# Gate and lift products of three branches with tokens on the output partitions

## The chip, the cores and the metric

One NeuronCore of a Trainium2 chip runs the whole program. The metric is the device time of one execution in microseconds (us). The engines are TensorE (PE; its weight loads are shown apart as PEld), VectorE (DVE), ScalarE (ACT), GpSimd (POOL) and SyncE (SP), which here issues the transfers of the weights.

## What is computed

Two encoder layers (DEPTH 2) on 256 tokens with a model width of 2048, in float32. A layer projects x, runs three token mixers (S5 scan, Hyena convolution, latent attention), each with 1024 channels, and merges them:

```
proj = x @ w_in[i]                      # 2048 wide into all branches, gates and PLE logits
y_a, y_b, y_c = three mixers, each times silu of its own part of proj      # 256 x 1024 each
gates  = sigmoid(gate_logits)           # 256 x 3 x 2048
lifted = y_n @ w_lift[n]                # 256 x 2048 for each branch n
mixed  = sum over n of gates_n * lifted_n, then @ w_out[i]
ple    = (p[i] @ w_ple[i]) * sigmoid(ple_logits)
x      = layer_norm(ALPHA * x + mixed + ple, ln_g[i], ln_b[i])
```

The change is in gates, lifted and the sum over the branches, and in how that sum reaches the product with w_out.

## The kernel before

**Weights.** All large weights come as 184 blocks a layer of 128 partitions x 2048 float32 (1 MB), in halves, through a ring of four half slots. ACT copies each quarter (128x512) of a block rounded to fp32r into WH (make_wh, L374), DVE subtracts it from the raw quarter into WL (make_wl, L388). x is held the same way as XH and XL (together XX), with channels on partitions and tokens as columns. A product is three fp32r matmuls: high x high, low x high, high x low. WH and WL hold one block; quarter q of the next block can be made only when TensorE is done with quarter q of this one (parts_used), so ACT and DVE run about three quarters ahead of TensorE at most.

**Narrow blocks.** A gate block holds the 2048 x 128 weights of 128 output channels. whole_block (through half_block, L1554) has the weight tile stationary and 256 tokens of x moving: 16 contraction tiles x 3 matmuls of 256 columns = 48 matmuls into one bank, channels on the output partitions. A lift block holds the 1024 x 128 weights of two output tiles: two half_block calls, again 48 matmuls of 256 columns. So the order of a layer is gate, gate, lift, eight times for each branch (24 blocks a branch, 48 gate and 24 lift blocks a layer).

**Merging.** For each pair of gate tiles ACT applies the sigmoid (into GA) from banks 0 and 1, and DVE multiplies by the lifts in banks 2 and 3. Branch A writes MIX; branches C and B multiply into LM and add to MIX (mix_in and its copy in the loop, L1058, L1060, L1114, L1116). MIX has channels on partitions.

**Stages of a layer**, in the order of each engine's hand-written program: S5 with the other projections; "lifta", where the 24 blocks of branch A are laid around the attention of eight heads (scores, block 3h, transposes of the probabilities, block 3h+1, product with V, block 3h+2); "hyc", 24 blocks of branch C around the Hyena filters and convolutions; "lift", 24 blocks of branch B in a hardware loop of two turns with little else; "ple", ten narrow blocks of the PLE logits and then 64 float32 matmuls for p @ w_ple; "out", the product with w_out; layer norm.

**Already wide.** The out stage has tokens on the output partitions: out_step takes 128 tokens of MIXH or MIXL as stationary tile and a 512-column quarter of WH or WL as moving one, 24 matmuls of 512 columns for a block, into banks 2g and 2g+1 for the two token halves. It takes MIX with channels on partitions; in "ple", ACT copies all of it to MIXH (L1461, 128x4096) after block 0 and DVE makes MIXL (L1122, 128x4096) after block 1. RES (ALPHA times x, L1126 and L1129) is made in four pieces at blocks 3 to 6.

**Between hyc and lift** ACT copies the Hyena result to YBH (L1441, 128x2048) and DVE makes YBL (L1098) before the weight splits of the second lift-stage block.

Of the kernel before, what the change touches and what calls it, by code (L numbers as in the profile page):

```python
# [27 lines left out]
F32 = mybir.dt.float32  # L28
# [6 lines left out]
P = 128  # L35
# [69 lines left out]
    "lifta": [8, 8, 8, 8, 0, 0, 0, 0],  # L105

    "hyc":  [8, 8, 8, 8, 18, 18, 20, 18],

    "lift": [8, 8, 8, 8, 0, 0, 0, 0],
    "ple":  [5, 5, 8, 8, 0, 0, 0, 0],  # L110
# [67 lines left out]
def trunk(nc, x, blocks, lp, ln, bc, w1, w2, b3, decay, feats, pT, pos, angles, consts, out):  # L178
    with ExitStack() as ctx:
# [103 lines left out]
        GA, LM = split(area(65, 2), 2), split(area(67, 2), 2)  # L283
        PTI = area(45, 2)
        MIXH, MIXL = parts("MIXH", 90, 16), parts("MIXL", 106, 16)
        RES = area(0, 16)
# [40 lines left out]
        mix_ready, ples_ready = sem("mix_ready"), sem("ples_ready")  # L327
# [91 lines left out]
        def _(pool):  # L419
# [7 lines left out]
            with pool.Fori(0, DEPTH) as layer:  # L427
# [27 lines left out]
                pool.wait_ge(yl_ready, layer * 4 + 1)  # L455
# [46 lines left out]
        def _(dve):  # L502
# [61 lines left out]
            with dve.Fori(0, DEPTH) as layer:  # L564
# [310 lines left out]
                dve.wait_ge(yh_ready, layer * 4 + 1)  # L875
                v.tensor_tensor(YAL, U, YAH.bitcast(F32), ALU.subtract).then_inc(yl_ready, 1)

                dve.wait_ge(yl_ready, layer * 4 + 1)
# [32 lines left out]
                for h in range(HEADS):  # L911
# [35 lines left out]
                    for b in range(2):  # L947
                        out_of(b, "lifta", h)
                        full(2 + b, "lifta", h)
                        free(v.tensor_tensor(split(MIX, DT)[:, 2 * h + b, :], GA[:, b, :], bank[2 + b][:, 0:T], ALU.mult), 2 + b)  # L950
                for b in (2, 3):
                    out_of(b, "lifta", 7)
# [99 lines left out]
                def mix_in(i, stage, n):  # L1052

                    for b in range(2):
                        mix = MIX[:, (2 * i + b) * T:(2 * i + b + 1) * T]
                        out_of(b, stage, n)
                        full(2 + b, stage, n)
                        free(v.tensor_tensor(LM[:, b, :], GA[:, b, :], bank[2 + b][:, 0:T], ALU.mult), 2 + b)  # L1058
                        out_of(2 + b, stage, n)
                        v.tensor_tensor(mix, mix, LM[:, b, :], ALU.add).then_inc(mix_ready, 1)  # L1060

                for k in range(24):
# [5 lines left out]
                    if s_ == 1 and o == 0:  # L1068

                        dve.wait_ge(yh_ready, layer * 4 + 2)  # L1070
                        v.tensor_tensor(YCL, YC, YCH.bitcast(F32), ALU.subtract).then_inc(yl_ready, 1)
# [20 lines left out]
                    if k % 3 == 2:  # L1092
                        mix_in(k // 3, "hyc", k // 3)
# [3 lines left out]
                dve.wait_ge(yh_ready, layer * 4 + 3)  # L1097
# [3 lines left out]
                with dve.Fori(0, 2) as turn:  # L1101
                    for k in range(12):
                        make_wl(dve, v, layer, B_LIFT + 48 + k + 1, turn, 12)
                        if k == 0:

                            dve.wait_ge(mix_ready, layer * 32 + 16)
                        if k % 3 < 2:
                            continue
                        for b in range(2):
                            i = k // 3  # L1110
                            mix = MIX[:, bass.ds(turn * (8 * T) + (2 * i + b) * T, T)]
                            out_of(b, "lift", i + turn * 4)
                            full(2 + b, "lift", i + turn * 4)
                            free(v.tensor_tensor(LM[:, b, :], GA[:, b, :], bank[2 + b][:, 0:T], ALU.mult), 2 + b)  # L1114
                            out_of(2 + b, "lift", i + turn * 4)
                            v.tensor_tensor(mix, mix, LM[:, b, :], ALU.add).then_inc(mix_ready, 1)  # L1116

                for m in range(10):
                    make_wl(dve, v, layer, B_PLE + m + 1)
                    if m == 1:  # L1120
                        dve.wait_ge(yh_ready, layer * 4 + 4)
                        v.tensor_tensor(MIXL, MIX, MIXH.bitcast(F32), ALU.subtract).then_inc(yl_ready, 1)  # L1122
                    if 3 <= m < 7:
                        half = slice((m % 2) * 8 * T, (m % 2 + 1) * 8 * T)
                        if m < 5:
                            st.did(v.tensor_scalar(RES[:, half], XH[:, half].bitcast(F32), ALPHA, None, ALU.mult))  # L1126
                        else:
                            st.wait()
                            st.did(v.scalar_tensor_tensor(out=RES[:, half], in0=XL[:, half].bitcast(F32), scalar=ALPHA, in1=RES[:, half],  # L1129
                                                          op0=ALU.mult, op1=ALU.add))  # L1130
# [86 lines left out]
        def _(act):  # L1217
# [11 lines left out]
            with act.Fori(0, DEPTH) as layer:  # L1229
# [153 lines left out]
                for h in range(HEADS):  # L1383
# [9 lines left out]
                    for b in range(2):  # L1393
                        for half in range(2):
                            make_wh(act, half, layer, lift_a(3 * h + 1 + b))
                        if h == b == 0:

                            act.wait_ge(qk_ready, layer * 2 + 2)
                        full(b, "lifta", h)

                        act.wait_ge(psum_free[2 + b], nth(layer, "lifta", 2 + b, h))
                        free(a.activation(GA[:, b, :], bank[b][:, 0:T], ACT.Sigmoid), b)
# [6 lines left out]
                for k in range(24):  # L1409
# [3 lines left out]
                    if k == 0:  # L1413

                        out_of(7, "mla", 7)
                        full(3, "lifta", 7)
# [16 lines left out]
                    b, i = k % 3, k // 3  # L1433
                    if b < 2:
                        full(b, "hyc", i)

                        act.wait_ge(psum_free[2 + b], nth(layer, "hyc", 2 + b, i))
                        free(a.activation(GA[:, b, :], bank[b][:, 0:T], ACT.Sigmoid), b)
# [4 lines left out]
                with act.Fori(0, 2) as turn:  # L1443
                    for k in range(12):
                        for half in range(2):
                            make_wh(act, half, layer, B_LIFT + 48 + k + 1, turn, 12)
                        b, i = k % 3, k // 3
                        if b < 2:
# [681 lines left out]
```

## Time and profile before

| | us |
|---|---|
| median of 3 runs | 2745.6 (2743.52 to 2748.16) |
| the profiled execution | 2739.96 |
| its span | 2737.7 |
| TensorE matmuls busy | 2634.4 (96%) |
| VectorE busy | 1886.8 (69%) |
| ScalarE busy | 1301.2 (48%) |
| mean granted TensorE clock | 0.985 |

Busy time of TensorE counts overlapped matmuls as one stretch, and the duration printed for one matmul includes its pipeline. The time that a matmul costs in a stream is therefore read from start to start. A timeline row is: start, duration, engine, line, operation, output <- inputs, shape, count, and in brackets the idle time before it and who ended it. A windows row is: stretch, its length, busy time and count for PE, PEld, DVE, ACT and POOL, the granted clock, the share of the DMA engines, GB/s.

### The profile page before, as it was taken

The page shows a single profiled execution, that of the slowest core. Times are in us where ns is not written, and L with a number is a line of the kernel's source. Part 1 is how long each engine was busy: PE and PEld are TensorE (multiplying, and loading weights), DVE is VectorE, ACT ScalarE, POOL GpSimd, SP SyncE. Part 2 cuts the span into 40 slices and gives each one's busy share as a digit, 9 for nine tenths or more (in the row PEclk, how much of TensorE's full clock was granted, in tenths as well). Part 3 has the DMA queues.
Part 4 walks back from the last instruction along what each step waited for, and adds up shares of the span by engine and source line. Part 5 has one row for each costly group of instructions (what it writes and reads, how often), then busy time and mean ns, then how long its engine had stood idle before and what let it go on. Part 6 is the DMA issues. An engine that isn't in the chain of part 4 may idle for free.

```text
span 2737.7 us, 48913 instructions
## 1 busy us (share of the span) xinstructions
PE 2634.4 (96%) x17128; PEld 2340.3 (85%) x17128; DVE 1886.8 (69%) x3381; ACT 1301.2 (48%) x2350; POOL 112.2 (4%) x206
## 2 busy tenths in 40 slices
PE   7999999999999999999989999999999999999998
PEld 6889999888987778998778999988799878789986
DVE  7788787635675767566678778786266757665666
ACT  5555555634543333453465555555355433344535
POOL 2100000000000000000030000000000000000000
PEclk9999999999999999999999999999999999999999
DMA  7444444334453324555464444443344523245554
GB/s 249 157 151 152 152 144 157 130 134 144 145 173 101 124 91 149 183 177 170 162 204 155 150 149 149 151 146 124 140 153 140 170 85 128 97 160 183 175 173 146
DMA packets 115978, 412.19 MB, mean 151 GB/s; under 512 B 15460, under 2 KB 15514, under 8 KB 115584
## 3 DMA queue, kind: packets, MB, share of 16 engines
q1 hardware_dynamic: 107424, 391.17, 43.0%
q0 software_dynamic: 8416, 19.18, 2.1%
q8 instruction: 88, 1.44, 0.2%
q14 instruction: 50, 0.41, 0.0%
HBM read 403.99 MB, written 6.29 MB: 150 GB/s over the span
## 4 chain that ended last, share of the span: by engine, by line
PE 86%; DVE 7%; issue 3%; ACT 2%; DMA 1%; PEldq 0%; PEld 0%; DVEq 0%; POOL 0%; POOLq 0%; ACTq 0%; SPq 0%
PE bank L1554 31%; PE bank L1582 19%; PE bank L1584 9%; PE bank L1924 6%; PE bank L1536 5%; PE bank L1672 2%; PE bank L1654 2%; PE bank L1635 2%; DVE WL L388 1%; PE bank L1845 1%; PE bank L1620 1%; PE bank L1740 1%; PE bank L1825 1%; PE bank L1807 1%; PE bank L1764 1%
## 5 line engine op out<-in xcount | busy, mean ns | idle before, releaser
L374 ACT ACTIVATE WH<-ring 128x512 fp32r<-128x512 f32 x1364 | 855.6, 631 | 1210.9 <-PE bank L1554 574.1
L388 DVE TENSOR_TENSOR WL<-ring,WH 128x512 fp32r<-128x512 f32 x852 | 571.1, 688 | 466.8 <-ACT WH L374 464.4
L1582 PE MATMUL bank<-XX,WH 128*128 128x512 f32 x2304 | 821.7, 400 | 26.7 <-DVE XX L557 15.2
L1554 PE MATMUL bank<-XX,WH 128*128 128x256 f32 x3712 | 687.4, 287 | 12.7 <-DVE WL L388 8.3
L1584 PE MATMUL bank<-XX,WL 128*128 128x256 f32 x2304 | 644.7, 280 | 0.0
L1554 PEld LDWEIGHTS bank<-XX,WH 128*128 128x128 f32 x3712 | 584.2, 194 | 31.4 <-issue 23.9
L1582 PEld LDWEIGHTS bank<-XX,WH 128*128 128x128 f32 x2304 | 436.0, 189 | 128.2 <-DVE XX L557 15.2
L1554 PE MATMUL bank<-XX,WL 128*128 128x256 f32 x1856 | 528.2, 285 | 0.0
L379 DVE TENSOR_TENSOR WL<-ring,WH 128x512 fp32r<-128x512 f32 x512 | 350.7, 687 | 137.8 <-ACT WH L374 133.8
L1584 PEld LDWEIGHTS bank<-XX,WL 128*128 128x128 f32 x2304 | 437.6, 190 | 0.0
L1554 PEld LDWEIGHTS bank<-XX,WL 128*128 128x128 f32 x1856 | 359.1, 193 | 0.0
L1536 PE MATMUL bank<-ARENA,ring 128*128 128x256 f32 x704 | 159.0, 388 | 13.9 <-ACT ARENA L1345 11.0
L1536 PEld LDWEIGHTS bank<-ARENA,ring 128*128 128x128 f32 x704 | 134.1, 194 | 38.4 <-issue 16.2
L1924 PE MATMUL bank<-WL,MIXH 128*128 128x512 f32 x256 | 101.9, 398 | 0.0
L1924 PE MATMUL bank<-WH,MIXH 128*128 128x512 f32 x256 | 101.1, 395 | 0.0
L1924 PE MATMUL bank<-WH,MIXL 128*128 128x512 f32 x256 | 101.0, 395 | 0.0
L1554 PE MATMUL bank<-YCH,WH 128*128 128x256 f32 x256 | 79.1, 309 | 0.0
L1554 PE MATMUL bank<-YCH,WL 128*128 128x256 f32 x256 | 75.0, 293 | 0.0
L1554 PE MATMUL bank<-YCL,WH 128*128 128x256 f32 x256 | 75.0, 293 | 0.0
L1554 PE MATMUL bank<-YAH,WH 128*128 128x256 f32 x256 | 75.0, 293 | 0.0
L1554 PE MATMUL bank<-YAH,WL 128*128 128x256 f32 x256 | 71.9, 281 | 0.0
L1554 PE MATMUL bank<-YAL,WH 128*128 128x256 f32 x256 | 71.9, 281 | 0.0
(305 smaller groups left out, 3492.4 us busy)
## 6 DMA issues: line engine op xcount, KB each, us to landing
ring<-in_blocks SPq DMA_DIRECT2D x738, 512.0 KB, 3.3
ARENA<-in_bc POOLq DMA_DIRECT2D x2, 2048.0 KB, 8.7
ARENA<-in_decay POOLq DMA_DIRECT2D x8, 512.0 KB, 4.3
ARENA<-in_x SPq DMA_DIRECT2D x4, 512.0 KB, 8.1
u_scratch<-ARENA POOLq DMA_DIRECT2D x16, 128.0 KB, 2.3
ARENA<-u_scratch POOLq DMA_DIRECT2D x64, 32.0 KB, 2.9
y_scratch<-ARENA POOLq DMA_DIRECT2D x16, 128.0 KB, 2.0
ARENA<-y_scratch POOLq DMA_DIRECT2D x64, 32.0 KB, 2.7
```

The source lines that it names most:

```text
L374: nc.scalar.activation(wh[q], raw(which[0], q), ACT.Copy).then_inc(wh_ready[q], 1)
L379: nc.vector.tensor_tensor(wl[q], raw(which[0], q), wh[q].bitcast(F32), ALU.subtract).then_inc(w_used[slot(which[0], q // 2)], 1)
L388: vec.tensor_tensor(wl[q], raw(which[0], q), wh[q].bitcast(F32), ALU.subtract).then_inc(w_used[slot(which[0], half)], 1)
L1536: ins = mm(o, w[:, (w0 + i) * P:(w0 + i + 1) * P], rhs(i), start=i == 0, stop=i == k - 1)
L1554: ins = mm(o, w_, x_, start=start and i == 0 and n == 0, stop=stop and i == 7 and n == 2)
L1582: ins = mm(bank[b][:, :], h, xx[:, :, k, :], start=(k == 0), stop=(k == DT - 1), skip_group_check=True)
L1584: ins = mm(bank[b][:, 0:T], l, xh[:, k, :], start=False, stop=(k == DT - 1), skip_group_check=True)
L1620: ins = nc.tensor.transpose(bank[b][:, i * P:(i + 1) * P], part_of(E, i % 2, i // 2, q, P), ident)
L1635: ins = mm(o, ET[:, q % 2 * CW + i * P:q % 2 * CW + (i + 1) * P], u4(q), start=True, stop=True)
L1654: ins = mm(bank[b][:, at:at + P], w_, f, start=(q % 2 == d == r == 0), stop=(q % 2 == d == r == 1), skip_group_check=True)
L1672: ins = mm(o, f, x_, start=False, stop=(d == 1 and r == 1))
L1924: ins = mm(bank[b][:, :], x_[:, k, tok[t]], w_[q], start=False, stop=(k == 15 and n == 2), skip_group_check=True)
```

## The change

Gate and lift products of the three branches take the form of the out stage. The host lays the weights out as blocks of four contraction tiles x 512 output channels (rows_by_cols). Output channels go in four groups of 512; a group has four gate blocks, accumulating in banks 0 and 1 (one for each half of the tokens), then two lift blocks in banks 2 and 3: six blocks in place of the six of two old rounds, and the same 24 blocks and bytes a branch. A block is token_block: for each quarter three matmuls of 512 columns for either token half, 24 in all. Sigmoid, product and sum work on 128x512 (two of each for six blocks, where four of 128x256 stood), and LM is gone: the product is written back to GA.

MIX now has tokens on partitions. 32 transposes a layer turn it back, 16 after PLE block 1 and 16 after block 4, four to a bank of banks 4 to 7. ACT rounds each bank into 512 columns of MIXH and DVE subtracts into MIXL, two banks at each of PLE blocks 2, 3, 5 and 6; the two 128x4096 operations are gone. The pieces of RES move to blocks 1, 4, 7 and 8, and the sigmoid of the first six PLE tiles from block 3 to block 7. The waits for YAL, YCL and YBL move from the third block of a branch to the fifth.

```diff
+                def token_step(b, x, k, t, q, first, last):
+
+                    hi, lo = (part[:, k, token[t]] for part in x)
+                    for n, (x_, w_) in enumerate(((hi, wh), (lo, wh), (hi, wl))):
+                        ins = mm(bank[b][:, :], x_, w_[q], start=first and n == 0, stop=last and n == 2)
+                        if n < 2:
+                            release(ins)
+                    return ins
+
+                def token_block(b, x, j, n, *which):
+
+                    for q in range(4):
+                        part_made(q, *which)
+                        k = 4 * j + q
+                        ins = [token_step(b + t, x, k, t, q, k == 0, k == 4 * n - 1) for t in range(2)]
...
+                def gated_block(stage, g, p, x, y, *which):
+
+                    b = 0 if p < 4 else 2
+                    if p in (0, 4):
+                        for t in range(2):
+                            take_bank(b + t, stage, g)
+                    token_block(b, y if b else x, p - 4 if b else p, 2 if b else 4, *which)
...
-                    take_bank(0, "lifta", h)
-                    whole_block(0, xh, xl, lift_a(3 * h))
+                    attention = lambda k: gated_block("lifta", k // 6, k % 6, (xh, xl), (split(YAH, WT), split(YAL, WT)), lift_a(k))
+                    attention(3 * h)
...
+                def mix_in(g):
+
+                    for t in range(2):
+                        out_of(t, "hyc", g)
+                        full(2 + t, "hyc", g)
+                        free(v.tensor_tensor(GA[:, t, :], GA[:, t, :], bank[2 + t][:, :], ALU.mult), 2 + t)
+                    for t in range(2):
+                        out_of(2 + t, "hyc", g)
+                        v.tensor_tensor(mix_part(g, t), mix_part(g, t), GA[:, t, :], ALU.add).then_inc(mix_ready, 1)
...
-                    if k % 3 == 2:
-                        mix_in(k // 3, "hyc", k // 3)
+                    if k % 6 == 5:
+                        mix_in(k // 6)
...
+                    if m in (1, 4):
+                        pe.wait_ge(mix_ready, layer * 16 + 16)
+                        for n in range(4 * (m // 4), 4 * (m // 4) + 4):
+                            b = 4 + n % 4
+                            take_bank(b, "ple", n // 4)
+                            for i in range(4):
+                                at = i % 2 * D + (2 * n + i // 2) * P
+                                ins = nc.tensor.transpose(bank[b][:, i * P:(i + 1) * P], MIX[:, at:at + P], ident)
...
+                        for n in mix_pairs[m]:
+                            full(4 + n % 4, "ple", n // 4)
+                            a.activation(MIXH[:, n * CW:(n + 1) * CW], bank[4 + n % 4][:, :], ACT.Copy).then_inc(mixh_ready, 1)
```

## Rows read from the trace of the kernel before

**Rows 1.** The page: busy time of the engines, chain that ended last by engine
```profile
PE 2634.4 (96%) x17128; PEld 2340.3 (85%) x17128; DVE 1886.8 (69%) x3381; ACT 1301.2 (48%) x2350; POOL 112.2 (4%) x206
PE 86%; DVE 7%; issue 3%; ACT 2%; DMA 1%; PEldq 0%; PEld 0%; DVEq 0%; POOL 0%; POOLq 0%; ACTq 0%; SPq 0%
```

**Rows 2.** Windows: two hyc gate blocks; a lift-stage round; four out blocks; ten PLE blocks
```profile
834.54:846.15 11.61, 11.61 (x98) 11.61 (x97) 8.31 (x13) 4.67 (x8) 0.98 (x2) 1.00 0.29 92
1088.83:1105.97 17.14, 17.14 (x146) 17.14 (x145) 9.65 (x17) 8.14 (x14) 0.00 (x0) 1.00 0.57 185
1292.37:1314.86 22.49, 22.49 (x99) 18.06 (x97) 13.76 (x28) 9.62 (x16) 0.00 (x0) 1.00 0.57 189
1193.59:1253.33 59.74, 58.31 (x481) 57.74 (x481) 39.17 (x49) 31.68 (x51) 0.00 (x0) 1.00 0.53 176
```

**Rows 3.** Timeline of PE, lift stage: first matmuls of gate pair, lift block, next pair
```profile
1088.83 0.40 PE L1554 MATMUL bank<-XX,WH 128*128 128x256 f32 x2
...
1100.34 0.28 PE L1554 MATMUL bank<-YBH,WH 128*128 128x256 f32 x1
...
1105.97 0.40 PE L1554 MATMUL bank<-XX,WH 128*128 128x256 f32 x2
```

**Rows 4.** Timeline of PE, out stage: first two matmuls of a group, next group's transposes
```profile
1292.37 0.48 PE L1924 MATMUL bank<-WH,MIXH 128*128 128x512 f32 x1
1292.69 0.40 PE L1924 MATMUL bank<-WH,MIXL 128*128 128x512 f32 x1
...
1314.86 0.49 PE L1939 MATMUL bank<-CON,ARENA 128*128 128x128 f32 x3
```

**Rows 5.** Timeline of PE, S5 stage: 512-column matmul on XX, the next matmul
```profile
204.11 0.39 PE L1582 MATMUL bank<-XX,WH 128*128 128x512 f32 x1
204.34 0.28 PE L1584 MATMUL bank<-XX,WL 128*128 128x256 f32 x1
```

**Rows 6.** Timeline of PE, attention: starts and ends of blocks 3h and 3h+2 of a head
```profile
651.88 0.50 PE L1554 MATMUL bank<-XX,WH 128*128 128x256 f32 x2
...
657.74 0.60 PE L1773 MATMUL bank<-CON,ARENA 128*128 128x128 f32 x4
...
664.60 0.47 PE L1554 MATMUL bank<-YAH,WH 128*128 128x256 f32 x1
...
670.49 0.38 PE L1763 MATMUL bank<-ARENA 128*128 128x256 f32 x1
```

**Rows 7.** Timeline of PE, S5 stage: 16 transposes and what follows them
```profile
90.66 1.89 PE L1635 MATMUL bank<-ARENA 128*128 x16
92.39 1.04 PE L1620 MATMUL bank<-CON,ARENA 128*128 128x128 f32 x8
```

**Rows 8.** Timeline of PE and of DVE where lift follows hyc
```profile
1055.15 0.80 PE L1554 MATMUL bank<-XX,WH 128*128 128x256 f32 x2 [2.82 <-DVE WL L388]
1060.23 0.36 PE L1554 MATMUL bank<-XX,WH 128*128 128x256 f32 x1 [0.50 <-DVE WL L388]
...
1055.62 0.41 DVE L1058 TENSOR_TENSOR ARENA<-ARENA,bank 128x256 f32<-128x256 f32 x1
...
1057.20 2.28 DVE L1098 TENSOR_TENSOR YBL<-ARENA,YBH 128x2048 fp32r<-128x2048 f32 x1
1059.40 0.68 DVE L388 TENSOR_TENSOR WL<-ring,WH 128x512 fp32r<-128x512 f32 x1
```

**Rows 9.** Timeline of DVE, lift stage: from the end of a round to the next splits
```profile
1106.96 0.69 DVE L388 TENSOR_TENSOR WL<-ring,WH 128x512 fp32r<-128x512 f32 x1 [0.77 <-ACT WH L374]
1107.57 0.41 DVE L1114 TENSOR_TENSOR ARENA<-ARENA,bank 128x256 f32<-128x256 f32 x1
...
1109.38 1.29 DVE L388 TENSOR_TENSOR WL<-ring,WH 128x512 fp32r<-128x512 f32 x2
```

**Rows 10.** Timeline of DVE and PE in ple: the large subtraction and who waits
```profile
1207.16 4.42 DVE L1122 TENSOR_TENSOR MIXL<-ARENA,MIXH 128x4096 fp32r<-128x4096 f32 x1
...
1212.33 0.47 PE L1554 MATMUL bank<-XX,WH 128*128 128x256 f32 x2 [0.85 <-DVE WL L388]
```

More of the change, by code:

```diff
@@ L946, in _ @@
                     short_conv(3 * h + 2)
[L947 to L950, printed above, removed]
+                    for t in range(2) if h % 2 else ():
+                        g = h // 2
+                        out_of(t, "lifta", g)
+                        full(2 + t, "lifta", g)
+                        free(v.tensor_tensor(mix_part(g, t), GA[:, t, :], bank[2 + t][:, :], ALU.mult), 2 + t)
                 for b in (2, 3):
-                    out_of(b, "lifta", 7)
+                    out_of(b, "lifta", 3)
                 out_of(7, "mla", 7)
@@ L1104, in _ @@
                         if k == 0:
-                            dve.wait_ge(mix_ready, layer * 32 + 16)
-                        if k % 3 < 2:
+                            dve.wait_ge(mix_ready, layer * 16 + 8)
+                        if k % 6 < 5:
                             continue
[L1109 to L1116, printed above, removed]
+                        i = k // 6
@@ L1784, in _ @@
                     done(ins, 7)
-                    if h == 0:
-                        pe.wait_ge(yl_ready, layer * 4 + 1)
-                    for i in range(2):
-                        take_bank(2 + i, "lifta", h)
-                        done(half_block(bank[2 + i][:, 0:T], i, split(YAH, WT), split(YAL, WT), True, True, lift_a(3 * h + 2)), 2 + i)
+                    attention(3 * h + 2)
                 settle()
@@ L1863, in inverse @@
                         done(ins, b)
-                def lift_blocks(stage, n, b, hi, lo, first, *which):
-                    if b < 2:
-                        take_bank(b, stage, n)
-                        whole_block(b, xh, xl, *which)
-                        return
-                    if first is not None:
-                        pe.wait_ge(yl_ready, first)
-                    for i in range(2):
-                        take_bank(2 + i, stage, n)
-                        done(half_block(bank[2 + i][:, 0:T], i, hi, lo, True, True, *which), 2 + i)
-                hi, lo = split(YCH, WT), split(YCL, WT)
+                yc = (split(YCH, WT), split(YCL, WT))
                 for k in range(24):
@@ L1894, in _ @@
                         inverse(o, s_ - 10)
-                    lift_blocks("hyc", k // 3, k % 3, hi, lo, layer * 4 + 2 if k == 2 else None, B_LIFT + 24 + k)
-                hi, lo = split(YBH, WT), split(YBL, WT)
+                    if k == 4:
+                        pe.wait_ge(yl_ready, layer * 3 + 2)
+                    gated_block("hyc", k // 6, k % 6, (xh, xl), yc, B_LIFT + 24 + k)
+                yb = (split(YBH, WT), split(YBL, WT))
                 settle()
```

154 lines of the change are left out of this document (90 added, 64 removed).

## Prediction

> **What bounds the kernel now.** First the page: matmuls keep TensorE busy for 96% of the span, it has 86% of the chain that ended last, VectorE 7% [rows 1]. So time is won where TensorE issues less or waits less, and work of ScalarE and VectorE counts only where TensorE stands waiting behind it. Then the windows of single stages, because the stages have different limits [rows 2]. In a round of the lift stage (gate, gate, lift) TensorE is busy for all of 17.14 us, VectorE for 9.65, ScalarE for 8.14, and the transfers take 0.57 of the DMA engines. The out stage looks the same with 22.49 us for four blocks and the same 0.57. The granted clock, the third column from the end, is 1.00 in both. Both are bounded by TensorE alone. In the ten PLE blocks 59.74 us hold only 58.31 of matmul time, so some waits stand there. Last, the timeline, start to start, for the price of one matmul, since the printed durations overlap.
>
> **The price of a block, narrow and wide.** In the lift stage a pair of gate blocks runs from 1088.83 to 1100.34, 11.51 us, 96 matmuls of 256 columns: 120 ns each, 5.755 us a block. The lift block runs from 1100.34 to 1105.97, 5.63 us, 48 matmuls: 117 ns each [rows 3]. The wide form exists in the out stage: 96 matmuls of 512 columns from 1292.37 to 1314.86. The first gap, 0.32 us, holds a switch from transposes of about 0.09; the rest is (22.49 - 0.09) / 96 = 233.3 ns each, 5.60 us for a block of 24 [rows 4]. Columns are the same in sum (48 x 256 = 24 x 512), so the gain is what a matmul costs above its columns: 5.755 - 5.60 = 0.155 us for a gate block and 0.03 for a lift block. The new instructions are those of the out stage in shape, order and moving operand; only the stationary tile is cut from XX, YAH, YBH or YCH, which no row shows. The price could be anything from 230 ns (the 512-column matmul with XX moving, 204.11 to 204.34 [rows 5]) to twice the gate's 120, 240. I take 233.3, the row nearest to the new form.
>
> The Trainium skill (TensorE: Matmul & The Clock Gate, "Wait — 56ns, not 53.3ns?") gives a warm matmul its columns at 2.4 GHz plus about 2.5 ns. By that two narrow ones would cost 2.5 ns more than one wide one, 0.06 us a block, 8.6 us for the 144 blocks. The trace gives 6.7 ns for a gate pair (2 x 120 - 233.3) and 1.3 for a lift pair, and neither width costs as little as the rule says. It returns beside a rival below.
>
> **Gain, stage by stage** (each number for both layers).
> - Lift stage: a round of 17.14 [rows 2] becomes 3 x 5.60 = 16.80, so 0.34 less, in 16 rounds: 5.4 us.
> - Attention: block 3h takes 651.88 to 657.74, 5.86 us, and block 3h+1, between the other two, 5.84; block 3h+2 takes 664.60 to 670.49, 5.89 [rows 6]. Above 48 matmuls these hold a switch from other work of 0.10, 0.08 and 0.26. With the out stage's 0.09 for the first two and 0.20 for the third, the new ones are 5.69, 5.69 and 5.80. That is 17.59 - 17.18 = 0.41 a head, in 16 heads: 6.6 us.
> - Hyc: a pair of gates between other work takes 11.61 [rows 2]; new 11.20 + 0.09, so 0.32 less, eight pairs' worth of gates a layer, 16 in both: 5.1 us. 16 lift blocks at 0.03 give 0.5. In two places of each layer TensorE stands for the last unconv of VectorE, which starts from the middle of a block; there half a block's gain (0.07) is lost, 0.2 in all. 5.4 us.
>
> Sum 17.4 us.
>
> **Added: 64 transposes.** In the S5 stage 16 float32 transposes take 90.66 to 92.39, 1.73 us, 108 ns each [rows 7]. A burst of 16 with one switch of 0.09 is 1.82, four bursts 7.3 us, all of it on TensorE in the PLE stage, where nothing hides it. The ends: the 275 ns that one of them is busy if nothing overlapped (1.89 - 15 x 0.108 = 0.27), 17.6 us, and about 6.4 at 100 ns. At the first burst TensorE also waits for the last sum into MIX, but two whole PLE blocks (11.5 us) lie ahead of it, and VectorE is done with the sums some 4 us after the lift stage; so nothing. The second burst needs banks 4 to 7 free again, read by VectorE at blocks 2 and 3, about 3 us after the end of block 3 and 2.5 before the transposes. Behind these waits only TensorE's own blocks are queued. The SP queue is not passed by any moved step; the blocks are as many and as large.
>
> **Removed: the large copies.** The copy to MIXH and the 4.42 us subtraction to MIXL hold back the splits of PLE block 2 and 3; TensorE waits, 0.85 us of it marked [rows 10]. Ten blocks at 5.755 would be 57.55 and they take 59.74 [rows 2]. Of the 2.2 left 0.7 is at the seam to the next stage (a wait for a transfer), and layer 1 has 59.12 without it, so 1.4 us a layer is the cost of the large operations: 2.8 us gained. In their place at blocks 2, 3, 5 and 6 stand two copies and two subtractions of 128x512, some 0.6 and 0.7 us each, behind the quarter that comes last (1.6 us after a block's end). The next quarter is then ready about 3.8 us after the block's end, and TensorE wants it at 5.76. The subtractions of RES (2.3 us each) sit at blocks 7 and 8, alone, as at 5 and 6 before. If this cover failed I would see TensorE idle there, up to the 1.4 us again.
>
> **Added: a longer stand at the seam from hyc to lift.** TensorE waits there on the low parts anyway, 2.82 and then 0.50 us (from 1059.57 to 1060.23 at the matmul starts) [rows 8]. VectorE's chain is: last splits, four sums of 128x256 (1055.62 to 1057.20, 1.58 us), YBL 2.2 us, split of the next block at 1059.40. Four operations of 128x512 at the 0.61 at which such splits follow each other take 2.5 us in place of 1.58: YBL, the split and TensorE come 0.9 later, in both layers 1.9 us lost. The move of the wait for YBL to the fifth block brings nothing: YBL is done 6 us before its old place.
>
> **Hidden: the sums elsewhere.** In the lift stage the last quarter's split ends at 1107.57, 1.60 us after the round ended (1105.97), four narrow operations take 1.81 and the next split starts at 1109.38 [rows 9]. Wide: 2.5 to 2.8 us, the next quarter ready at 1110.7 to 1111.0, wanted at 1105.97 + 5.60 = 1111.57. At least 0.5 us of cover is left. In attention the products end 0.5 us later ahead of every second softmax, which has over a microsecond in hand; the sigmoids fall on every second head alone.
>
> **The sum.** -17.4 + 7.3 - 2.8 + 1.9 = -11.0 us. Against the profiled execution, 2739.96, that is 2729.0. It lies 5.6 below the median; in the same ratio the median of 2745.6 becomes 2734.6.
>
> **Rivals.**
> - Width gives less on XX: a wide matmul there costs 236.6 ns, halfway between the out stage's 233.3 and twice the gate's 120. That is 2304 x 3.3 ns = 7.7 us less gain, 2742.3. For it: the lift blocks, already at 117 ns, gain next to nothing. Against: the out stage [rows 4] and XX moving at 230 [rows 5]. Chance 0.09. The Trainium skill's rule from the section named above ends near the same time by another road, 8.6 us of gain in place of 17.4 and so 2743.4; the traces speak against it, since neither width has its gap here.
> - XX as an operand costs 120 ns for 256 columns wherever it stands, so its wide matmul costs 240. Its place: the 96 gate blocks, 2304 matmuls, 6.7 ns each: 15.4 us more than forecast, 2750.0, slower than before. It turns from faster to slower at 238 ns. For it: YBH in the same loop has 117 where XX has 120. Against: XX moving over 512 columns takes 230 [rows 5]. Chance 0.07.
> - The wide sums use up their cover, and TensorE waits at every sixth block of hyc and lift (16 places); this decides from a chain of 3.3 us, and at 0.5 us each it costs 8: 2742.6. Chance 0.06.
> - More stands go than I count (softmax chain, PLE blocks, switches as cheap as 0.09 everywhere, a seam hidden), 6 us more: 2728.6. Chance 0.10.
> - The clock falls in other places: after the stand of 2.82 us a pair of matmuls shows 0.80 us where others have 0.40 to 0.50 [rows 8, 3], the lower of the two levels (1.2 GHz). One more or one less in each layer moves the time by 3 to 4 us either way, inside the range.
> - The change not doing what it says is ruled out by its diff: every narrow block of the three branches is replaced.
>
> **Chances.** The forecast has 0.68, and of it 0.95 lies below the bound. 0.2% of the median, about what a measurement of this kernel can tell from no change, is 5.5 us: faster means below 2740.1. Faster: 0.65 + 0.10 = 0.75, and a small part of the two middle rivals, 0.77. Slower by over 0.2% (above 2751.1): a third of the second rival and what I have not thought of, 0.05. Same: 0.18. The range that leaves out 2 in 10 is 2728 to 2743.
>
> **What would show it.** In the changed trace: 512-column matmuls on XX 233 ns apart and a lift-stage group of six blocks in 33.6 us (two old rounds: 34.3); 16 transposes in about 1.7 us, twice a layer; no wait for a split within the PLE blocks; the first wait of the lift stage unchanged and the second one near 1.5 us in place of 0.66; every six-block end without a wait. The forecast is wrong if matmuls on XX are 237 ns or more apart, if the transposes take over 3 us a burst, or if TensorE waits for low parts behind the wide sums.

## The result, and the profile after

| us | before | after |
|---|---|---|
| median (range, runs) | 2744.85 (2743.52 to 2748.16, 4) | 2709.48 (2707.26 to 2712.84, 4) |
| the profiled execution | 2739.96 | 2707.26 |
| its span | 2737.7 | 2705.7 |
| TensorE matmuls busy | 2634.4 | 2605.2 |

The ratio is 0.9874, 95% interval 0.9861 to 0.9886: 35 us faster, between 31 and 38. The forecast was 2734.6, 11 us faster, and its range ended at 2728. The sign was right and the size a third of what came.

The page of the changed kernel, the same two lines as [rows 1]: busy time, then the chain that ended last.

```profile
PE 2605.2 (96%) x13736; PEld 2160.3 (80%) x13736; DVE 1882.6 (70%) x3315; ACT 1275.7 (47%) x2300; POOL 111.3 (4%) x206
PE 90%; DVE 5%; issue 2%; ACT 2%; DMA 1%; PEldq 0%; PEld 0%; DVEq 0%; POOL 0%; POOLq 0%; ACTq 0%
```

TensorE is still the bound, with 3392 fewer matmuls. Windows of the changed kernel (columns as in [rows 2]): four gate blocks of the lift stage, two lift blocks, four out blocks, the ten PLE blocks with the transposes, the first four gate blocks after the seam, the taps behind hyc block 2, then the stages attention, hyc of layer 0 and hyc of layer 1.

```profile
1075.17:1096.98 21.81, 21.81 (x98) 18.02 (x96) 13.19 (x21) 10.12 (x16) 0.00 (x0) 1.00 0.61 193
1131.24:1142.44 11.20, 11.20 (x49) 9.01 (x48) 5.57 (x9) 5.92 (x10) 0.00 (x0) 1.00 0.52 188
1253.13:1275.61 22.48, 22.48 (x100) 18.05 (x98) 12.46 (x28) 9.49 (x15) 0.00 (x0) 1.00 0.60 188
1176.23:1237.40 61.17, 61.16 (x512) 61.17 (x513) 40.93 (x56) 31.90 (x58) 0.00 (x0) 1.00 0.52 169
1035.98:1063.97 27.99, 24.04 (x96) 18.88 (x97) 20.29 (x33) 11.06 (x17) 1.09 (x2) 0.94 0.49 157
822.19:828.66 6.47, 5.61 (x18) 2.12 (x17) 3.50 (x6) 0.63 (x1) 0.00 (x0) 1.00 0.46 156
626.81:798.47 171.66, 170.83 (x739) 132.91 (x739) 123.61 (x262) 81.94 (x146) 1.58 (x3) 1.00 0.47 154
798.47:1035.98 237.51, 225.15 (x928) 159.58 (x929) 169.09 (x275) 79.75 (x126) 4.64 (x9) 0.98 0.35 117
2137.68:2377.02 239.34, 226.99 (x928) 160.74 (x929) 169.08 (x275) 79.74 (x126) 4.63 (x9) 0.97 0.35 115
```

Windows of the kernel before, the last three of these stages.

```profile
625.62:802.45 176.83, 175.88 (x1315) 162.84 (x1315) 122.75 (x270) 92.54 (x162) 1.58 (x3) 1.00 0.46 149
802.45:1049.20 246.75, 232.15 (x1504) 192.80 (x1505) 171.77 (x291) 80.94 (x134) 4.64 (x9) 0.97 0.34 113
2158.79:2407.31 248.52, 233.92 (x1504) 193.47 (x1505) 171.76 (x291) 80.91 (x134) 4.64 (x9) 0.97 0.34 112
```

Two rows stand out. Four gate blocks take 21.81 us, 96 matmuls, 227.2 ns each; two lift blocks take 11.20, 48 matmuls, 233.3 ns each. Same shape, same code line, same moving operands WH and WL; only the stationary tile differs, XX or YBH. The forecast had 233.3 for both. And hyc lost 9.2 us in each layer, far above what its blocks explain.

Cutting both traces at the same instructions gives the ledger (both layers, us, after less before):

| stage | forecast | measured |
|---|---|---|
| S5 and layer norm between the layers | 0 | +1.0 |
| attention | -6.6 | -10.4 |
| hyc | -5.4 | -18.4 |
| lift, seam included | -5.4 + 1.9 | -8.3 |
| ple | +7.3 - 2.8 | +3.5 |
| the rest | 0 | +0.6 |
| span | -11.0 | -32.0 |

Timeline of the changed kernel: the release in hyc (PE, then ACT), the transposes, the seam (PE and DVE).

```profile
822.19 1.12 PE L1861 MATMUL bank<-ARENA 64*128 64x512 f32 x2
823.15 1.02 PE L1862 MATMUL bank<-ARENA,CON 64*128 64x512 f32 x2
825.03 1.14 PE L1861 MATMUL bank<-ARENA 64*128 64x512 f32 x4 [0.86 <-DVE ARENA L1003]
...
822.29 0.63 ACT L380 ACTIVATE WH<-ring 128x512 fp32r<-128x512 f32 x1 [0.59 <-PE bank L1599]
...
1187.84 1.91 PE L1962 MATMUL bank<-CON,ARENA 128*128 128x128 f32 x16
1189.51 0.48 PE L1574 MATMUL bank<-XX,WH 128*128 128x256 f32 x2
...
1041.71 0.74 PE L1599 MATMUL bank<-WH,XX 128*128 128x512 f32 x2 [2.73 <-DVE WL L394]
1047.52 0.73 PE L1599 MATMUL bank<-WH,XX 128*128 128x512 f32 x2 [1.22 <-DVE WL L394]
...
1042.17 1.28 DVE L1064 TENSOR_TENSOR ARENA<-ARENA,bank 128x512 f32<-128x512 f32 x2
1044.57 2.29 DVE L1105 TENSOR_TENSOR YBL<-ARENA,YBH 128x2048 fp32r<-128x2048 f32 x1
```

And of the kernel before, the same place in hyc (PE, then ACT).

```profile
827.02 1.12 PE L1807 MATMUL bank<-ARENA 64*128 64x512 f32 x2
827.99 1.02 PE L1808 MATMUL bank<-ARENA,CON 64*128 64x512 f32 x2
830.92 1.14 PE L1807 MATMUL bank<-ARENA 64*128 64x512 f32 x4 [1.91 <-DVE ARENA L996]
...
828.18 0.63 ACT L374 ACTIVATE WH<-ring 128x512 fp32r<-128x512 f32 x1 [1.66 <-PE bank L1807]
```

Before, the block ended at 827.02, but ACT could make the last quarter of the next block only at 828.18: a block's last quarter was released by the next matmul that carries a release (`pending`), here a 512-column float32 matmul of the filter taps. VectorE's split waits for ACT, its taps work queues behind that split, and TensorE stood for it 1.91 us. After, the gate block's own last matmul releases the quarter; ACT starts at 822.29, 0.10 behind the block, and TensorE stands 0.86 us. The stretch from 827.02 to 834.54, whose row stands below, took 7.52 us; in the changed kernel it takes 6.47. That is 1.05 us at each of four places: all four stands of this kind (two in each layer) are 1.91 before and 0.86 after.

```profile
827.02:834.54 7.52, 5.61 (x17) 2.12 (x16) 5.09 (x10) 0.63 (x1) 0.00 (x0) 1.00 0.42 139
```

The diff had it all along, in the `else` of token_block, and the prediction does not price it.

### The profile page after: what moved, and what is told of

It reads as the page before. It is cut to its first block, busy times and chain, and to the rows that moved or that the text cites. A ratio compares the mean times of both kernels' runs of the same rounds, so it can differ in the third digit from the quotient of the medians.

```text
span 2705.7 us, 41637 instructions
## 1 busy us (share of the span) xinstructions
PE 2605.2 (96%) x13736; PEld 2160.3 (80%) x13736; DVE 1882.6 (70%) x3315; ACT 1275.7 (47%) x2300; POOL 111.3 (4%) x206
## 4 chain that ended last, share of the span: by engine, by line
PE 90%; DVE 5%; issue 2%; ACT 2%; DMA 1%; PEldq 0%; PEld 0%; DVEq 0%; POOL 0%; POOLq 0%; ACTq 0%
PE bank L1599 28%; PE bank L1639 19%; PE bank L1641 10%; PE bank L1979 6%; PE bank L1556 5%; PE bank L1574 4%; PE bank L1729 2%; PE bank L1711 2%; PE bank L1692 2%; PE bank L1899 2%; PE bank L1797 1%; PE bank L1677 1%; PE bank L1879 1%; PE bank L1821 1%; PE bank L1913 1%
## 5 line engine op out<-in xcount | busy, mean ns | idle before, releaser
L1641 PE MATMUL bank<-XX,WL 128*128 128x256 f32 x2304 | 644.4, 280 | 0.0
L1639 PEld LDWEIGHTS bank<-XX,WH 128*128 128x128 f32 x2304 | 435.8, 189 | 129.3 <-issue 15.6
L1599 PE MATMUL bank<-WH,XX 128*128 128x512 f32 x1536 | 495.2, 404 | 11.7 <-DVE WL L394 8.3
L1641 PEld LDWEIGHTS bank<-XX,WL 128*128 128x128 f32 x2304 | 437.6, 190 | 0.0
L1599 PEld LDWEIGHTS bank<-WH,XX 128*128 128x128 f32 x1536 | 290.7, 192 | 91.5 <-issue 22.3
L1599 PE MATMUL bank<-WL,XX 128*128 128x512 f32 x768 | 304.9, 397 | 0.0
L1599 PEld LDWEIGHTS bank<-WL,XX 128*128 128x128 f32 x768 | 147.5, 192 | 32.2
L1574 PE MATMUL bank<-XX,WH 128*128 128x256 f32 x640 | 115.9, 284 | 1.3 <-issue 1.3
L1574 PEld LDWEIGHTS bank<-XX,WH 128*128 128x128 f32 x640 | 99.7, 192 | 2.1 <-issue 2.1
L1574 PE MATMUL bank<-XX,WL 128*128 128x256 f32 x320 | 90.5, 283 | 0.0
L1729 PE MATMUL bank<-ARENA 128*128 128x64 f32 x512 | 67.6, 275 | 0.0
L1711 PE MATMUL bank<-ARENA 128*128 128x128 f32 x512 | 62.3, 275 | 0.0
```

The lines of the kernel that those rows point to most:

```text
L1574: ins = mm(o, w_, x_, start=start and i == 0 and n == 0, stop=stop and i == 7 and n == 2)
L1599: ins = mm(bank[b][:, :], x_, w_[q], start=first and n == 0, stop=last and n == 2)
L1639: ins = mm(bank[b][:, :], h, xx[:, :, k, :], start=(k == 0), stop=(k == DT - 1), skip_group_check=True)
L1641: ins = mm(bank[b][:, 0:T], l, xh[:, k, :], start=False, stop=(k == DT - 1), skip_group_check=True)
L1711: ins = mm(bank[b][:, at:at + P], w_, f, start=(q % 2 == d == r == 0), stop=(q % 2 == d == r == 1), skip_group_check=True)
L1729: ins = mm(o, f, x_, start=False, stop=(d == 1 and r == 1))
```

## The experiments

Two theories on the 21 us that the forecast lacked. **Theory P (place):** a wide matmul with XX stationary is cheaper than one with YBH or MIXH, because of where the operands lie. In SBUF, XX, WH and WL begin at multiples of 64 bytes and ARENA, which holds YBH and MIXH, 32 bytes beyond one; YAH and YCH lie in ARENA too. Two operands are called in line below when both begin at the same place against 64 bytes. **Theory R (release):** hyc gained from the earlier release. Rivals: the stationary tile's own layout or stage sets the price, and hyc gained from the width alone. The recorded expectations letter their theories A, B and C, each run anew; A is the place in the first two.

**a_arena64: the changed kernel, ARENA moved on by 32 bytes.**

```diff
+        arena_pad = sb("arena_pad", 8)
         arena_at = nc.sbuf_base
```

> The changed kernel with 32 bytes of padding ahead of ARENA, so that ARENA (YAH, YBH, YCH, MIXH and all else in it) starts at a multiple of 64 bytes in each partition, where it started at 32 beyond one; XX starts at a multiple of 64 in both. Theory A (the stationary tile's place against 64 bytes sets the price: 227 ns from XX, 233 from ARENA): lift blocks and the out stage go from 233.3 to 227 ns a matmul, (1152 + 768) x 6.1 ns = 11.7 us less than the changed kernel, some 2698 us against its 2709.5. Theory B (XX is cheaper for another reason: its region of the SBUF, or what else runs beside it): 233 ns stay, same time.

Measured: 2712.84 (2707.81 to 2713.28), 0.9878 [0.9855, 0.99] of before, where 2698 was expected. Windows: four gate blocks, two lift blocks, four out blocks.

```profile
1084.58:1106.34 21.76, 21.76 (x98) 18.02 (x97) 13.20 (x21) 10.11 (x16) 0.00 (x0) 1.00 0.58 194
1140.35:1151.34 10.99, 10.99 (x50) 9.02 (x48) 5.56 (x9) 5.92 (x10) 0.00 (x0) 1.00 0.58 190
1261.72:1283.80 22.08, 22.08 (x100) 18.07 (x99) 12.36 (x28) 9.48 (x15) 0.00 (x0) 1.00 0.57 191
```

The lift pair falls from 11.20 to 10.99 (229 ns a matmul), four out blocks from 22.48 to 22.08. It does not become XX's 227, so place is not the whole of it. The total shows none of the gain. In the profiled execution the S5 stages (with the layer norm between the layers) were 3.0 and 2.6 us longer, and attention and the lift stage of layer 0, which had more time at the lower clock, 2.5 and 2.0 longer. That ARENA's place lengthened S5 is not shown: in a_shift below, which leaves ARENA where it is, the same stages are 2.1 and 2.4 us longer, and in a_turn2, which moves nothing, 1.2 and 2.1.

**a_xx32: the changed kernel, XX moved on by 32 bytes.** The two paddings together move what comes behind XX by 64 bytes, so all else keeps its place against 64 bytes.

```diff
+        xx_before = sb("xx_before", 8)
         XX = sb("XX", 2 * DT * T, dt=F32R)
+        xx_after = sb("xx_after", 8)
```

> The changed kernel with XX moved to 32 bytes beyond a multiple of 64, ring, WH, WL and ARENA as they were against 64. Theory A: gate blocks go from 227 to 233 ns a matmul, 2304 x 6.1 ns = 14 us more, some 2723 us. The narrow PLE blocks, where XX moves, may go from 120 to the 117 ns that YBH had when it moved (960 matmuls, 3 us less). Theory B: no change, 2709.

Measured: 2730.52 (2727.76 to 2732.67), 0.9949 [0.9928, 0.9969]. Windows: gates, lifts.

```profile
1086.35:1108.75 22.40, 22.40 (x97) 18.00 (x96) 13.21 (x21) 10.12 (x16) 0.00 (x0) 1.00 0.56 188
1075.15:1086.35 11.20, 11.20 (x49) 9.01 (x48) 5.54 (x9) 5.92 (x10) 0.00 (x0) 1.00 0.58 189
```

The gates now cost 233.3 ns, the very number of the forecast, and the lifts are untouched. The median rose by 21 us, the span by 23.3. The three stages with the gates account for 13.7 of it (worked out: 96 blocks x 24 x 6.1 ns = 14.1), S5 for 10.8, and the PLE blocks gave 1.6 back. The projections of S5 have XX as moving operand, but since S5 was up to 4.5 us longer with XX in place (a_shift), not all of the 10.8 need be XX's. The windows settle the larger part of the miss.

**a_wh32: the changed kernel, WH and WL moved on by 32 bytes, XX and ARENA as they were against 64.** Is it the place of each operand, or how the two lie to one another?

```diff
+        wh_before = sb("wh_before", 8)
         WH, WL = sb("WH", BLK, dt=F32R), sb("WL", BLK, dt=F32R)
+        wl_after = sb("wl_after", 8)
```

> The changed kernel with WH and WL 32 bytes further on and everything else where it was: the same instructions, only the place of the split weights against 64 bytes is new. Theory A (each operand counts by its own place, and the stationary tile is what matters for a wide matmul): the wide gate blocks keep their 227 ns (four of them 21.8 us), lift blocks their 233; the weights moving from a displaced WH cost nothing, and the time is 2709 +- 5. Theory B (what counts is how stationary and moving operand lie to each other): XX now differs from WH and goes to 233 ns (22.4 us for four blocks), YBH and MIX now agree with it and go to about 227 (lift block pair 10.9 us, out 96.0): the gates lose 96 x 0.15 = 14 us, lifts and out gain 48 x 0.15 + 3, so some 2713. Theory C (the moving operand counts by itself): every wide matmul of gates, lifts and out becomes slower by 3 to 6 ns, 3456 + 768 of them, 13 to 25 us: 2722 to 2735.

Measured: 2727.13 (2723.23 to 2728.25), 0.9933 [0.9916, 0.9949]. Windows: gates, lifts, out.

```profile
1089.03:1111.43 22.40, 22.40 (x97) 18.02 (x96) 13.20 (x21) 10.15 (x16) 0.00 (x0) 1.00 0.56 187
1146.33:1157.33 11.00, 11.00 (x50) 9.03 (x48) 5.53 (x9) 5.93 (x10) 0.00 (x0) 1.00 0.53 190
1267.57:1289.64 22.07, 22.07 (x100) 18.08 (x98) 12.36 (x28) 9.50 (x15) 0.00 (x0) 1.00 0.58 191
```

These are theory B's rows (it had 22.4, 10.9 and 96.0 for the whole out stage, which took 96.1): XX had not moved against 64 bytes and went from 21.81 to 22.40; YBH and MIXH had not moved either and went to 11.00 and 22.07. So the price follows how the two operands lie to each other. The time is 14 us above theory B's 2713. S5 (+5.0 and +5.1 us) was not in the expectation, although a_xx32 had shown it, and hyc and the lift stage took up to 4.6 us a layer more, with more time at the lower clock (mean granted clock of the whole 0.982 against 0.985).

**b_xx32 and b_arena64: the same two moves in the kernel before**, the first three lines in the one, the last two in the other.

```diff
+        xx_before = sb("xx_before", 8)
         XX = sb("XX", 2 * DT * T, dt=F32R)
+        xx_after = sb("xx_after", 8)
...
+        arena_pad = sb("arena_pad", 8)
         arena_at = nc.sbuf_base
```

> The kernel before with XX 32 bytes beyond a multiple of 64. It fills the fourth field of a table: 256-column matmuls on XX cost 120 ns at a multiple of 64 as moving operand, 512-column ones with XX stationary 227 there and 233 beside it. If the moving XX gets cheaper beside it (117 to 118, as YBH had and as the PLE blocks of a_xx32 show), the width is worth only 2 x 118 - 233 = 3 ns a pair there, against 13 at the multiple. If it stays at 120, it is worth 7. Gate blocks go from 5.755 to 5.65 us or stay; the 512-column matmuls of S5 may cost some 5 us a layer more, as in a_xx32, so the total may rise.

> The kernel before with ARENA at a multiple of 64. Theory A: the out stage's 768 matmuls go to 227 ns, 4.7 us less; the narrow lift blocks, where ARENA moves, may go from 117 to the 120 ns of XX, 2304 x 2.5 ns = 5.8 us more: about the same time, 2744, with both prices changed. Theory B: nothing changes.

Measured: b_xx32 2752.33 (2744.93 to 2756.97), 1.001 [0.9996, 1.0023]; b_arena64 2740.05 (2736.72 to 2748.64), 0.9986 [0.9969, 1.0004]. Neither total can be told from the kernel before; the windows can. Windows of b_xx32 (two narrow gate blocks) and of b_arena64 (the same, then a narrow lift block).

```profile
1080.54:1091.90 11.36, 11.36 (x98) 11.36 (x97) 6.89 (x13) 5.33 (x9) 0.00 (x0) 1.00 0.58 188
```

```profile
1076.90:1088.40 11.50, 11.50 (x98) 11.50 (x97) 6.95 (x13) 5.33 (x9) 0.00 (x0) 1.00 0.54 187
1088.40:1093.86 5.46, 5.46 (x50) 5.46 (x49) 2.69 (x5) 2.80 (x5) 0.00 (x0) 1.00 0.54 188
```

The narrow form does not follow the wide one. With XX displaced against WH a narrow gate matmul is cheaper, 118.3 against 119.8 ns, where a wide one is dearer. YBH goes the other way: in line with WH it is 113.7, displaced 117 [rows 3], where the expectation had a rise to 120. So for gates the change is worth 239.6 - 227.2 = 12.4 ns for each wide matmul in these kernels and 236.6 - 233.3 = 3.3 with XX displaced. Had I priced it from a kernel laid out otherwise, I would have read another gain.

**a_late and a_late2: the changed kernel with the old release.** a_late gives the last quarter of each block (and the second) to `pending` again, everywhere; a_late2 only the last one, and only at hyc blocks 2 and 14, where the taps follow; its condition is `late and q == 3` in place of the one below.

```diff
+                        elif q % 2:
+                            release(ins[0])
+                            pending.append((parts_used[q], 1))
                         else:
                             release(ins[0])
                             ins[1].then_inc(parts_used[q], 1)
```

> The changed kernel, but the release of the last quarter of every block is put on the next matmul but one that takes one, as in the kernel before, in place of the block's own last matmul. Theory: at blocks 2 and 14 of hyc the next matmuls are 512 columns of float32, so the release, the last split and the unfold behind it come 1.05 us later, four times: 4 us more, with one clock window more or less 2 to 8, 2712 to 2717 us. Rival (the earlier start of unfold comes from the missing sums at those blocks): same time, 2709.5.

> The changed kernel, with the release of the last quarter put off to the next matmul that takes one at hyc blocks 2 and 14 alone. Theory: the float32 matmuls that follow put the release off by 1.05 us, and split, unfold and the next matmuls with it: 4 x 1.05 = 4.2 us more on its own, with clock windows at 1.2 GHz added up to 10 us; hyc goes from 237.5 and 239.3 us to 240 or more. Rival (a_late lost its 20 us at the other blocks): under 1 us.

Measured: a_late 2729.38 (2721.78 to 2734.72), 0.9934 [0.9909, 0.996], well beyond its expectation. a_late2 2723.35 (2717.39 to 2730.36), 0.9917 [0.9894, 0.994]. Timeline row and windows of a_late2: the taps, hyc of both layers. The profiled execution is the fastest of its four.

```profile
826.04 1.86 PE L1864 MATMUL bank<-ARENA 64*128 64x512 f32 x4 [1.91 <-DVE ARENA L1003]
...
822.15:831.37 9.22, 7.31 (x18) 2.74 (x17) 3.50 (x6) 0.63 (x1) 0.00 (x0) 0.81 0.31 110
798.40:1041.70 243.30, 228.85 (x928) 160.82 (x929) 169.05 (x275) 79.78 (x126) 4.63 (x9) 0.96 0.34 114
2143.42:2386.69 243.27, 228.82 (x929) 160.93 (x929) 169.07 (x275) 79.81 (x126) 4.63 (x9) 0.96 0.34 113
```

Windows of a_late: hyc of layer 0.

```profile
798.70:1049.61 250.91, 235.57 (x929) 164.64 (x929) 169.44 (x276) 80.47 (x126) 4.63 (x9) 0.94 0.34 111
```

The stand of 1.91 us is back to the hundredth, at all four places, so the release is its cause. But the stretch took 9.22 us against 6.47: 1.05 by the wait and 1.7 because behind the longer stand the granted clock fell (0.81 over the stretch, 1.00 after the change; 0.19 of 9.22 is the 1.75). Hyc grew by 5.8 and 3.9 us in the two layers, of which 2 x 1.05 each is the wait; the rest, 3.7 and 1.8, goes with a mean clock of 0.96 against 0.98 and 0.97. In a_late the clock has 0.94: 0.04 of 251 us is about 10 of the 13.4 lost in layer 0. This second payment was in both expectations, up to 10 us in a_late2's, which held, and too small in a_late's. Before the change such a fall did not follow this particular stand (1.00 in 827.02 to 834.54), so a stand of this length does not by itself bring one; that it makes one likelier is argued from these two runs and not shown.

**a_turn2: the changed kernel, each transpose made twice.**

```diff
-                            for i in range(4):
+                            for i in (0, 1, 2, 3, 0, 1, 2, 3):
```

> The changed kernel with every one of the 64 transposes of MIX issued twice into the same place. My price, now read as 104 ns each from the changed kernel's trace, says 64 x 0.104 = 6.7 us more, 2716 us, all in the PLE stage (61.2 to 64.5 us a layer). Rival (the transposes stand beside waits for splits, so part of them is hidden): less than 3 us more.

Measured: 2717.39 (2715.86 to 2722.75), 0.9885 [0.9866, 0.9904], 7.9 us above the changed kernel. Timeline: one burst.

```profile
1192.25 3.65 PE L1962 MATMUL bank<-CON,ARENA 128*128 128x128 f32 x32
1195.66 0.48 PE L1574 MATMUL bank<-XX,WH 128*128 128x256 f32 x2
```

32 in 3.41 us, so sixteen more cost 1.75, and the four bursts 7.0. The PLE stages grew from 61.17 to 64.66 us, so nothing hides the transposes, as forecast.

**b_pieces: the kernel before, MIXH and MIXL made in eight pieces.** Only this part of the change: one 128x512 copy and one subtraction at each of eight PLE blocks in place of the two 128x4096 ones.

```diff
-                        v.tensor_tensor(MIXL, MIX, MIXH.bitcast(F32), ALU.subtract).then_inc(yl_ready, 1)
+                    if 1 <= m < 9:
...
+                        dve.wait_ge(mixh_ready, layer * 8 + (n + 1))
+                        ins = v.tensor_tensor(MIXL[:, pair], MIX[:, pair], MIXH[:, pair].bitcast(F32), ALU.subtract)
```

> The kernel before with the two 128x4096 operations (copy to MIXH, subtraction to MIXL) cut into eight of 128x512 each, one at each of PLE blocks 0 to 7 and 1 to 8; nothing else changed. Theory: the 1.4 us a layer that TensorE waits at PLE blocks 2 and 3 go away, 2.8 us less than the kernel before, PLE stage 59.7 and 59.1 to about 58 us. Rival (those waits have another cause, such as a transfer): no change.

Measured: 2744.78 (2737.39 to 2748.71), 0.9988 [0.9974, 1.0001]. Windows: the ten PLE blocks, hyc of layer 0.

```profile
1196.60:1254.28 57.68, 57.68 (x480) 57.68 (x481) 39.62 (x56) 31.90 (x58) 0.00 (x0) 1.00 0.54 180
802.14:1052.25 250.11, 235.47 (x1505) 194.45 (x1505) 171.93 (x291) 80.93 (x134) 4.63 (x9) 0.96 0.34 111
```

In the stage TensorE no longer waits: 59.7 and 59.1 us became 57.7, a gain of 2.0 and 1.4. The total hides it: hyc of layer 0, which the edit does not touch, took 250.1 us in place of 246.8, at a clock of 0.96 in place of 0.97.

**a_shift, a_flat, a_best: can the place be used?** a_shift moves YBH, YBL, MIXH and MIXL, not the rest of ARENA, by 32 bytes (and the small STATS by 1 KB, to make room). a_flat writes the lift stage's loop of two turns out, which drops its loop gaps, and puts mix_in(3), YBH and YBL of hyc behind the splits of the second lift-stage block. a_best does both.

```diff
-            return nc.alloc_sbuf_tensor_at(name, [P, n * T], F32R, offset=arena_at + at * T * 4)[:]
+            return nc.alloc_sbuf_tensor_at(name, [P, n * T], F32R, offset=arena_at + at * T * 4 + by)[:]
...
-        MIXH, MIXL = parts("MIXH", 90, 16), parts("MIXL", 106, 16)
+        MIXH, MIXL = parts("MIXH", 90, 16, 32), parts("MIXL", 106, 16, 32)
...
-                with pe.Fori(0, 2) as turn:
+                for turn in range(2):
```

> The changed kernel with only YBH, YBL, MIXH and MIXL moved by 32 bytes, to a multiple of 64, ARENA and XX left as they are. Theory A: the out stage costs 96.0 us a layer in place of 97.6, the lift blocks of branch B 227 to 229 ns a matmul in place of 233; S5 keeps its time, which rose by 3 us a layer when all of ARENA moved. 2 x 1.6 + 768 x 0.005 = 7 us less than the changed kernel, 2702.5. Rival (place against 64 bytes is not what counts there): 2709.5.

> The changed kernel with the two-turn loops of the lift stage written out on TensorE, VectorE and ScalarE, and with mix_in(3), YBH and YBL placed after the splits of the second lift-stage block. Theory: the wait of 1.5 us at the start of that block goes (the seam was priced at 0.9 us a layer for the wide sums and had 0.7 before), 3 us for both layers; the matmul gaps at the loop's entry, turn and exit (0.7, 1.2 and 0.8 us) go, 5 us: 2701.5. Rivals: instruction fetch of the longer program takes the loop's gain back (2706); only the splits of the first block, which wait for unconv, count, so the seam gives nothing (2704.5).

> a_shift and a_flat together: if their gains add, 2694 to 2696 us; if the clock's windows fall differently, up to 5 us either way.

Measured: a_shift 2706.13 (2699.79 to 2709.51), 0.9853 [0.9835, 0.9872]; a_flat 2706.87 (2705.03 to 2707.66), 0.986 [0.9845, 0.9875]; a_best 2699.46 (2698.19 to 2703.21), 0.9832 [0.9819, 0.9846]. Windows of a_shift: gates, lifts, out.

```profile
1077.31:1099.07 21.76, 21.76 (x97) 18.02 (x96) 13.20 (x21) 10.11 (x16) 0.00 (x0) 1.00 0.59 194
1133.16:1144.14 10.98, 10.98 (x49) 9.02 (x48) 5.54 (x9) 5.91 (x10) 0.00 (x0) 1.00 0.58 192
1254.54:1276.61 22.07, 22.07 (x100) 18.07 (x98) 12.36 (x28) 9.48 (x15) 0.00 (x0) 1.00 0.57 191
```

Windows of a_best: the first gates after the seam, a lift pair, the rest of the lift stage, out.

```profile
1037.34:1067.10 29.76, 24.91 (x98) 19.74 (x96) 20.89 (x36) 11.72 (x17) 1.09 (x2) 0.89 0.48 154
...
1067.10:1078.09 10.99, 10.99 (x50) 9.02 (x49) 5.56 (x9) 5.92 (x10) 0.00 (x0) 1.00 0.64 196
...
1099.85:1176.33 76.48, 76.48 (x338) 63.09 (x337) 43.06 (x65) 38.08 (x62) 0.00 (x0) 1.00 0.58 193
1253.46:1275.53 22.07, 22.07 (x99) 18.08 (x98) 12.35 (x28) 9.51 (x15) 0.00 (x0) 1.00 0.57 191
```

Both edits do what they should in their stages: aligned prices (10.99, 22.07) and a lift stage without a gap (PE busy for all of 76.48 us, where the changed kernel has 12.37 and 11.98 for two of its lift pairs). a_best is the fastest kernel here, 10 us below the changed one. a_shift and a_flat alone cannot be told from the changed kernel, since their intervals overlap its 0.9861 to 0.9886.

a_shift missed its 2702.5 by 3.6: in the profiled execution out and lift gained 3.2 and 1.9 us and S5 was 4.5 longer, so that the span is the changed kernel's. a_flat missed its 2701.5 by 5.4 and a_best its 2694 to 2696 by 3, inside the 5 us that it gave the clock. A part of both shows: the first gates after the seam took 29.76 us at a clock of 0.89, against 27.99 at 0.94, and TensorE stands there 3.70 us in one piece, where the changed kernel has 0.71 and 2.73 at two places. Whether the later sums there bring that about or chance does is open; writing the loops out without moving the sums was not tried.

## Why the prediction was wrong in size

**The price of the wide gate matmul: the step that failed.** I took 233.3 ns from the out stage [rows 4] and gave 230 to 240 as its bounds, from XX moving over 512 columns [rows 5]. It is 227.2, outside them. The row I chose had the right shape and moving operand and the wrong relative place: in the out stage the stationary tile lies 32 bytes off the moving one, for the gates they are in line. a_xx32 and a_wh32 show it from both sides. It is worth 96 x 24 x 6.1 ns = 14.1 us, a third of it in each of attention, hyc and lift. Narrow gates cost 120 as read, so the gain is 0.30 us a block and not 0.155. The lower bound should have stood lower: nothing in the trace of before showed XX stationary with WH moving, and one size of one other pair is no floor.

**The release of the last quarter: a step that was missing.** 4 x 1.05 = 4.2 us, shown by a_late2. In the text I listed what moves on ACT and DVE and did not read which matmul carries `parts_used`.

**The clock in hyc.** In hyc of layer 0 the trace has three stretches at the lower level (1.2 GHz) where it had four; in layer 1 it has four before and after, and one that was twice as long as the others became like them. Half of the time that went from the lower level is 1.7 us a layer, 3.4 in all, if TensorE had work throughout it. The forecast had such a move as a rival of 3 to 4 us either way; the size was right. That shorter stands bring it is made likely by a_late2, not shown for each stretch.

These make -11.0 - 14.1 - 4.2 - 3.4 = -32.7 against -32.0 by the spans. By stage: attention -6.6 - 4.7 = -11.3 (measured -10.4), hyc -5.4 - 4.7 - 4.2 - 3.4 = -17.7 (-18.4), lift -3.5 - 4.7 = -8.2 (-8.3). The 0.9 in attention and the 0.7 in hyc, of opposite sign, stay unplaced.

**Right, with their measures.**
- Lift blocks at 233.3 ns: 11.20 for 48. Their gain is next to nothing, as said.
- The transposes, by luck in their price: 16 in 1.66 us (1187.84 to 1189.51), forecast 1.82; a_turn2 gives 1.75. The row of [rows 7] that gave 108 ns (L1635) holds no transposes: it is the S5 stage's product of ET with 64 columns of U4. The transposes there are the eight of the line below it (L1620), 92.39 to the next matmul at 93.19, 100 ns each. That they stand bare in the PLE stage was right for the reason given.
- The large copies: b_pieces gains 2.0 and 1.4 us in the two layers, forecast 1.4 each. In the changed kernel 61.17 less twice 1.66 leaves 57.85 for ten blocks, without a wait, as against 59.74 [rows 2].
- The seam: four wide sums take 1042.17 to 1044.57, 2.40 us (forecast 2.5), the first wait of TensorE is 2.73 (2.82 before), the second 1.22 (forecast near 1.5). The first four gate blocks took 27.99 us, 6.18 above 21.81; in the kernel before the first pair took 16.85 (1049.20 to 1066.05), 5.34 above 11.51. That is 0.84 a layer, forecast 0.9.
- Cover of the wide sums: behind the seam TensorE waits for no split in the lift stage, and for none in hyc of either layer; the rival of sixteen waits is out.

**The rivals.** XX at 236.6 or 240 is out, since the miss lay on the other side. "More stands go" had the right direction for hyc and was sized at 6 us; with the clock it holds 7.6. The Trainium skill's rule (TensorE: Matmul & The Clock Gate, "Wait — 56ns, not 53.3ns?") gives, as an estimate, 2.5 ns for a pair of gate matmuls and 8.6 us for the whole. The traces disagree, with 12.4 ns for a gate pair in these kernels and 3.3 with XX displaced: a rule without the operands' places cannot give both.

## What to carry to other kernels

Price a new instruction from a row with the same two operands, or widen the bound by what other pairs of the same shape differ by; here 6.1 ns of 233.3 on one matmul were worth 14.1 us, more than the whole forecast gain. Read for every quarter and buffer which instruction carries the release before and after: a release that hung on the next, slower matmul cost 1.05 us at each of four places here, and more where the clock fell as well. A total of one profile can hide a stage's gain (b_pieces), so judge an edit by its stage's window at the same granted clock, and only then by the median.

## What the runs showed of the hardware

Start-to-start price in ns of one warm fp32r matmul (granted clock 1.00) from the windows, by whether the stationary and the moving operand begin at the same place against 64 bytes or 32 bytes apart:

| pair and size | in line | 32 bytes apart |
|---|---|---|
| XX stationary, 512 columns of WH/WL moving | 227 | 233 |
| YBH stationary, the same | 229 | 233 |
| MIXH stationary, the same (with its switch) | 230 | 234 |
| WH stationary, 256 columns of XX moving | 120 | 118 |
| WH stationary, 256 columns of YBH moving | 114 | 117 |

No operand's own place decides: in a_wh32 XX and YBH stayed and their prices moved in opposite directions as WH moved. For the wide form in line is cheaper in all three; the narrow form with XX is the exception, and why is open. Other distances than 32 bytes were not tried, nor the places of YAH and YCH alone.
